# Retention: the first head's query handled inside the norm, values ahead of context keys, weight splits behind the rows that wait

## What is computed

```
hn, gn = pre_norm(h), pre_norm(g)              # latent, context
q = rotary(hn @ Wq);  k = rotary(hn @ Wk) / 16;  v = hn @ Wv;  gate = hn @ Wg
k_c = gn @ Wk / 16;   v_c = gn @ Wv
per head (4 heads, key width 256, value width 512):
    s_fwd, s_bwd = decayed sums of k_c x v_c   # state from the context
    o = scan(q, k, v, decay 0, s_fwd) + flipped scan(q, k, v, decay 1, s_bwd, strict)
    y = groupnorm(o) * gain * silu(gate);  h += mod * (y @ Wo)
```

## Time and profile before

| | us |
|---|---|
| median of 3 timed runs | 3056.75 (3056.71 to 3057.57) |
| the profiled execution | 3057.61 |
| its span | 3055.9 |

### The profile page before, as it was taken

How to read it: one execution, slowest core, us unless ns; L and a number is a source line. 1 busy time by engine, 2 the same in 40 slices (tenths; PEclk the granted TensorE clock), 3 DMA queues, 4 the chain that set the end, 5 groups by cost and what they waited for, 6 DMA issues and landing times.

```text
span 3055.9 us, 42286 instructions
## 1 busy us (share of the span) xinstructions
PE 2994.7 (98%) x17472; PEld 2608.9 (85%) x17472; DVE 1806.0 (59%) x2615; ACT 859.9 (28%) x1150; POOL 37.3 (1%) x74
## 2 busy tenths in 40 slices
PE   7999999999999999999999999999899999999999
PEld 5888888888898888888888888888788888888887
DVE  5765555766667775555673565658464646464454
ACT  5111121354445411121241121213332322332221
POOL 0000000000000000000000000000000000000000
PEclk9999999999999999999999999999999999999999
DMA  6332332111110333232311232321121212112222
GB/s 266 140 131 100 110 110 96 55 53 56 56 53 31 148 126 112 110 106 100 110 70 56 96 110 96 110 96 68 42 83 42 74 49 83 55 70 96 96 96 83
DMA packets 41064, 278.08 MB, mean 91 GB/s; under 512 B 4368, under 2 KB 5648, under 8 KB 8080
## 3 DMA queue, kind: packets, MB, share of 16 engines
q1 hardware_dynamic: 31024, 205.85, 18.6%
q0 software_dynamic: 9952, 70.98, 6.5%
HBM read 274.72 MB, written 2.10 MB: 91 GB/s over the span
## 4 chain that ended last, share of the span: by engine, by line
PE 90%; DVE 6%; ACT 2%; issue 1%; DMA 1%; SPq 0%; POOL 0%; DVEq 0%; ACTq 0%; POOLq 0%
PE ps L330 29%; PE ps L332 28%; PE ps L331 28%; PE ps L652 1%; PE ps L356 1%; DVE wl L1372 1%; DVE act_buf L1456 1%; DVE xnl L1460 1%; ACT wh L965 1%; DMA ada_w<-ada 1%; PE ps L344 1%; PE ps L638 0%; DMA adaw<-ada 0%; PE ps L639 0%; ACT xnh L996 0%
## 5 line engine op out<-in xcount | busy, mean ns | idle before, releaser
L330 PE MATMUL ps<-xnh,wl 128*128 128x512 f32 (+1 forms) x3040 | 1058.2, 348 | 12.3 <-DVE wl L1372 5.5
L331 PE MATMUL ps<-xnl,wh 128*128 128x512 f32 (+1 forms) x3040 | 1048.4, 345 | 0.0
L332 PE MATMUL ps<-xnh,wh 128*128 128x512 f32 (+1 forms) x3040 | 1047.5, 345 | 0.0
L330 PEld LDWEIGHTS ps<-xnh,wl 128*128 128x128 f32 x3040 | 577.2, 190 | 95.0 <-issue 10.7
L332 PEld LDWEIGHTS ps<-xnh,wh 128*128 128x128 f32 x3040 | 577.0, 190 | 70.1
L331 PEld LDWEIGHTS ps<-xnl,wh 128*128 128x128 f32 x3040 | 577.4, 190 | 67.7 <-issue 1.0
L965 ACT ACTIVATE wh<-raw 128x2048 fp32r<-128x2048 f32 (+2 forms) x176 | 322.7, 1834 | 560.8 <-PE ps L332 560.8
L1372 DVE TENSOR_TENSOR wl<-raw,wh 128x2048 fp32r<-128x2048 f32 (+1 forms) x178 | 393.6, 2211 | 139.8 <-ACT wh L965 139.6
L1529 DVE SCALAR_TENSOR_TENSOR h<-ps,coef,h 128x512 f32<-128x512 f32 x624 | 371.3, 641 | 106.1 <-PE ps L332 104.7
L330 PE MATMUL ps<-hidh,wl 128*128 128x512 f32 (+1 forms) x1232 | 422.4, 343 | 3.5 <-DVE h L1471 3.3
L332 PE MATMUL ps<-hidh,wh 128*128 128x512 f32 (+1 forms) x1232 | 423.2, 344 | 0.0
(11 more groups left out here) (255 smaller groups left out, 2973.4 us busy)
## 6 DMA issues: line engine op xcount, KB each, us to landing
raw<-weights SPq DMA_DIRECT2D x183, 1024.0 KB, 4.8
adaw<-ada POOLq DMA_DIRECT2D x64, 1024.0 KB, 5.0
ada_w<-ada SPq DMA_DIRECT2D x8, 1024.0 KB, 19.2
h<-x_in SPq DMA_DIRECT2D x1, 2048.0 KB, 8.7
c_act<-c_rows POOLq DMA_DIRECT2D x2, 1024.0 KB, 5.8
out<-h SPq DMA_DIRECT2D x8, 256.0 KB, 2.0
h<-x_in SPq DMA_DIRECT2D x1, 1024.0 KB, 28.9
cs<-rope_mla POOLq DMA_DIRECT2D x1, 512.0 KB, 3.7
```

The source lines that it names most:

```text
L330: mm(dst, lhs[1][rows], rhs[0][rows], start=first, stop=False)
L331: mm(dst, lhs[0][rows], rhs[1][rows], start=False, stop=False)
L332: return mm(dst, lhs[0][rows], rhs[0][rows], start=False, stop=last)
```

## The change

The first head's query is split, rotated and split again **between the two parts of the norm** instead of behind both: `last_y` gets a function `between`, which ScalarE calls ahead of `norm_hi` of part 1 and VectorE ahead of `normed` of part 1. In the first head TensorE multiplies **two value sets ahead of the context keys**, the second of them into bank 0, since bank 7 still holds the norm's spread; a wait for the query (`qk_ready`) stands in front of it. VectorE and ScalarE take the latent keys and the first value ahead of the decays, and the second value and the context keys behind them. Latent and context keys signal `qk_full` apart. In **all heads** ScalarE makes the context keys' high halves ahead of the split of the second value weights, VectorE makes the first value's low half ahead of that split and the decays' add, and the split of the gate weights stands behind the scores on both engines. The buffers `rk`, `st`, `rv`, `rq` change places, so that `rq` no longer lies over the norm's `act_buf`.

The diff; `rotate` is moved out of `head` unchanged and left out, as are the functions that hand `between` on and the loops' counts:

```diff
         mla_mem.close()
         ret_mem = ExitStack()
+        rk = sb("rk", [P, 2, 2, T], F32R, ret_mem)
+        st = sb("st", [P, 2, 6, S], F32R, ret_mem)
+        rv = sb("rv", [P, 2, 6, 256], F32R, ret_mem)
         rq = sb("rq", [P, 2, 2, S], F32R, ret_mem)
-        rk = sb("rk", [P, 2, 2, T], F32R, ret_mem)
-        rv = sb("rv", [P, 2, 6, 256], F32R, ret_mem)
-        st = sb("st", [P, 2, 6, S], F32R, ret_mem)
...
-                for i, (t0, n) in enumerate(STREAMS):
+                def keys(part):
+
+                    t0, n = STREAMS[part]
                     for j in range(2):
                         for k in range(KD):
-                            if first and not i and j and k == 4:
+                            if first and not part and j and k == 4:
                                 norm_spread(1)
-                            if first and i and j == 0:
+                            if first and part and j == 0:
                                 pe.wait_ge(xn_ready, c.next(xn_ready))
-                            ins = three(ps[:, 2 + 2 * i + j, 0:n], w(s1, k * 256 + j * P), xn(k, t0, n), k == 0, k == KD - 1)
-                        if first and i == 0 and j == 0:
+                            ins = three(ps[:, 2 + 2 * part + j, 0:n], w(s1, k * 256 + j * P), xn(k, t0, n), k == 0, k == KD - 1)
+                        if first and not part and j == 0:
                             norm_sums(1)
-                ins.then_inc(qk_full, 1)
+                    ins.then_inc(qk_full, 1)
+                keys(0)
+                if not first:
+                    keys(1)
                 pe.wait_ge(w_ready[s0], c.next(w_ready[s0]))
                 values(s0, 6, 0)
-                values(s0, 7, 1)
+                if first:
+                    pe.wait_ge(qk_ready, c.next(qk_ready))
+                    values(s0, 0, 1)
+                    keys(1)
+                else:
+                    values(s0, 7, 1)
                 pe.wait_ge(v_ready, c.next(v_ready))
                 values(s0, 6, 2)
-                pe.wait_ge(qk_ready, c.next(qk_ready, 2))
+                pe.wait_ge(qk_ready, c.next(qk_ready, 2 if first else 3))
+                if first:
+                    pe.wait_ge(v_ready, c.next(v_ready))
                 for jc in range(6):
                     if jc >= 4:
...
-                pe.wait_ge(v_ready, c.next(v_ready, 2))
+                pe.wait_ge(v_ready, c.next(v_ready, 1 if first else 2))
...
                 norm_root(1, parts)
+                if between is not None:
+                    between()
                 for m in range(KD):
...
-            slot = ffn(2, slot, (1, 1))
-
-
-            s0, s1 = slot, 1 - slot
...
+            def first_query():
+                act.wait_ge(qk_full, c.next(qk_full))
+                split_hi(1 - slot)
+                for j in range(2):
+                    part(qk_val, qk_hi, rq[:, 0, j, :], rt[:, j, :])
+            slot = ffn(2, slot, (1, 1), between=first_query)
+
+
+            s0, s1 = slot, 1 - slot
...
-                act.wait_ge(qk_full, c.next(qk_full))
-                split_hi(s0)
-                for j in range(2):
-                    part(qk_val, qk_hi, rq[:, 0, j, :], rt[:, j, :])
+                def ctx_keys():
+                    act.wait_ge(qk_full, c.next(qk_full))
+                    fn(rk[:, 0, 0, S:T], ps[:, 4, 0:L], ACT.Copy)
+                    fn(rk[:, 0, 1, S:T], ps[:, 5, 0:L], ACT.Copy).then_inc(qk_hi, 1)
+
+                def rows(kind):
+                    for j in range(2):
+                        part(qk_val, qk_hi, kind(j), rt[:, j, :])
+
+                def value(t):
+                    bank = 0 if first and t == 1 else 6 + t % 2
+                    part(v_full, v_hi, rv[:, 0, 2 * t:2 * t + 2, :], two_tiles(bank))
+                first = isinstance(i, int) and i == 0
+                if first:
+                    act.wait_ge(qk_full, c.next(qk_full))
+                    rows(lambda j: rk[:, 0, j, 0:S])
+                    value(0)
+                else:
+                    act.wait_ge(qk_full, c.next(qk_full))
+                    split_hi(s0)
+                    rows(lambda j: rq[:, 0, j, :])
                 act.wait_ge(dec_done, c.next(dec_done))
                 fn(dec_lat, dec_lat, ACT.Exp)
                 fn(dec_ctx, dist[:, L:DIST_W], ACT.Exp, bias=lg[:, 5, at(i)], scale=lgf)
                 fn(far[:], dist[:, L:DIST_W], ACT.Exp, bias=lg[:, 6, at(i + RET_HEADS)], scale=nlgb).then_inc(dec_exp, 1)
-                act.wait_ge(qk_full, c.next(qk_full))
-                split_hi(s1)
-                fn(rk[:, 0, 0, S:T], ps[:, 4, 0:L], ACT.Copy)
-                fn(rk[:, 0, 1, S:T], ps[:, 5, 0:L], ACT.Copy).then_inc(qk_hi, 1)
-                for j in range(2):
-                    part(qk_val, qk_hi, rk[:, 0, j, 0:S], rt[:, j, :])
-                for t in range(3):
-                    part(v_full, v_hi, rv[:, 0, 2 * t:2 * t + 2, :], two_tiles(6 + t % 2))
-                split_hi(s0)
+                if first:
+                    value(1)
+                    ctx_keys()
+                    split_hi(s1)
+                else:
+                    act.wait_ge(qk_full, c.next(qk_full))
+                    ctx_keys()
+                    split_hi(s1)
+                    rows(lambda j: rk[:, 0, j, 0:S])
+                    value(0)
+                    value(1)
+                value(2)
                 for jc in range(6):
                     part(sc_val, sc_hi, st[:, 0, jc, :], rt[:, jc % 2, :])
+                split_hi(s0)
                 act.wait_ge(o_full, c.next(o_full, 2))
                 for t in range(3):
                     part(v_full, v_hi, rv[:, 0, 2 * t:2 * t + 2, :], two_tiles(2 + t % 2))
...
@@ -1518,6 +1559,8 @@
                 inverse_rms(1, parts)
                 if early is None:
                     gate_coefs(layer, k)
+                if between is not None:
+                    between()
                 normed(1, layer, k, parts)
 
...
+            def query(s):
                 dve.wait_ge(qk_full, c.next(qk_full))
-                split_lo(s0)
+                split_lo(s)
                 rotate(0)
                 for j in range(2):
                     dve.wait_ge(qk_hi, c.next(qk_hi))
                     ins = tt(rq[:, 1, j, :], rt[:, j, :], rq[:, 0, j, :].bitcast(F32), ALU.subtract)
                 ins.then_inc(qk_ready, 1)
...
+            def first_query():
+                dve.wait_ge(tab_full, 48)
+                query(1 - slot)
+            slot = ffn(2, slot, (1, 1), ADA_2, between=first_query)
...
+                def ctx_keys():
+                    dve.wait_ge(qk_full, c.next(qk_full))
                     dve.wait_ge(qk_hi, c.next(qk_hi))
-                    ins = tt(rk[:, 1, j, 0:S], rt[:, j, :], rk[:, 0, j, 0:S].bitcast(F32), ALU.subtract)
-                ins.then_inc(qk_ready, 1)
-                split_lo(s1)
-                dve.wait_ge(dec_exp, c.next(dec_exp))
-                step(tt(dec_ctx, dec_ctx, far[:], ALU.add))
+                    for j in range(2):
+                        ins = tt(rk[:, 1, j, S:T], ps[:, 4 + j, 0:L], rk[:, 0, j, S:T].bitcast(F32), ALU.subtract)
+                    ins.then_inc(qk_ready, 1)
+
+                def other_keys():
+                    dve.wait_ge(qk_full, c.next(qk_full))
+                    dve.wait_ge(qk_ready, c.next(qk_ready, 1 if first else 2))
+                    rotate(2)
+                    for j in range(2):
+                        dve.wait_ge(qk_hi, c.next(qk_hi))
+                        ins = tt(rk[:, 1, j, 0:S], rt[:, j, :], rk[:, 0, j, 0:S].bitcast(F32), ALU.subtract)
+                    ins.then_inc(qk_ready, 1)
...
-                for t in range(3):
-                    value(t, 6 + t % 2)
-                split_lo(s0)
-                dve.wait_ge(qk_ready, c.next(qk_ready))
+                first = isinstance(i, int) and i == 0
+                if not first:
+                    query(s0)
+                else:
+                    other_keys()
+                    value(0, 6)
+                step(ts(dec_lat, dist[:], nlgb, None, ALU.mult))
+                stt(out=dec_lat, in0=dist[:], scalar=lgf, in1=dec_lat, op0=ALU.mult, op1=ALU.min).then_inc(dec_done, 1)
+                if first:
+                    value(1, 0)
+                    ctx_keys()
+                else:
+                    ctx_keys()
+                    other_keys()
+                    value(0, 6)
+                split_lo(s1)
+                dve.wait_ge(dec_exp, c.next(dec_exp))
+                step(tt(dec_ctx, dec_ctx, far[:], ALU.add))
+                if not first:
+                    value(1, 7)
+                value(2, 6)
+                dve.wait_ge(qk_ready, c.next(qk_ready, 2 if first else 1))
...
@@ -1912,6 +1978,7 @@
                         dve.wait_ge(sc_hi, c.next(sc_hi))
                         tt(st[:, 1, jc - 1, :], rt[:, (jc - 1) % 2, :], st[:, 0, jc - 1, :].bitcast(F32),
```

(50 more changed lines are left out.)

14 lines of the change are left out of this document (2 added, 12 removed).

## The result

| | before | after |
|---|---|---|
| median us (4 runs each) | 3056.73 (3055.35 to 3057.57) | 3028.98 (3028.00 to 3030.22) |
| ratio | | 0.9913, 95% interval 0.9902 to 0.9925 |
| the profiled execution, us | 3057.61 | 3029.51 |
| its span | 3055.9 | 3027.9 |

Faster by 27.7 us.

A forecast was written before the change was run, and what follows sets the result against it. TensorE, busy 98% of the span, was taken as the bound, so only its gaps could be won. First head 15.3 plus other heads 7.7 made 23.0 us, giving 3034 us; range 3032 to 3041.5.

The forecast's parts named there:

- The first head: Term for the first head: moving the query and reordering TensorE brings its fifth score block 15.3 us earlier.
- The wait for the first value: First head, TensorE waiting for the low half of `rv`: 10.2 us, forecast to shrink to about 0.1.
- the chain of ten pieces: First head, VectorE and ScalarE durations added in program order: scores at 2161.3, with a new 0.5 us wait before them.
- the pause of 1.3 us: First head, TensorE's pause before the fifth score block: 1.3 us by the trace, forecast to stay.
- The low clock: First head, third value set slowed at 1.2 GHz after the pause: 2.3 us lost, forecast to be recovered.
- The other heads: Heads two to four: waits for the first value and before the fifth score block go, 2.6 us each, 7.7 in all.
- the extra signal: Separate signal for the keys, forecast to cost nothing that a row could show.
- from the sum to the time: Last step: 23.0 us off the profiled 3057.61, then 0.86 off for the median: 3033.8, say 3034.
- (a): Rival, chance 0.10: only the first head gains, another wait takes over in the steady heads; 3041.4 us.
- (b): Rival, chance 0.07: the first head's chain is longer than added up; 6 us longer, with low clock, gives 3042 us.
- (c): Rival, chance 0.03: the value wait just becomes the same wait for context keys; 3056.75 us or a little less.
- (d): Rival, chance 0.04: slower, the first head's delayed second norm part becomes the bound; about 3063 us.

The follow-up runs named there:

- e6: Changed kernel, but in the first head TensorE takes the context keys ahead of the two value sets again; median 3039.23 us, ratio 0.9951.
- e3: Kernel before the change, with 42 never-read products filling TensorE's 10.2 us pause in the first head; median 3051.84 us, ratio 0.9992.
- e1: Changed kernel with only the first head's edits, heads two to four in the order of before; median 3041.3 us, ratio 0.9952.
- e5: Changed kernel keeping only the gate-weight split behind the scores in heads two to four, all else in the old order; median 3049.51 us, ratio 0.9986.
- e10: The changed kernel run a third time, nothing altered; median 3030.45 us, ratio 0.9919.
- e2: Changed kernel with the first head back in the order of before, heads two to four as changed; median 3046.84 us, ratio 0.9972.
- e7: Changed kernel, but the first head's query is handled behind both parts of the norm; TensorE's new order stays; median 3039.61 us, ratio 0.9951.

## Why the prediction was right or wrong

**The first head: right.** The query block took 2131.12 to 2138.70, 7.6 us (7.65 forecast), and nothing on its way was slower than in its old place. The norm's second part was put off by 5.9 us against the latent keys (6.1), with no wait on TensorE; e6 shows what the cover is worth, 7.7 us. The wait for the first value is gone. The term is 0.45 us too small, nearly all of it ahead of the scores. They start 35.98 us behind the first key product, and 2161.3 - 2124.93 = 36.4 had been forecast: the chain of ten pieces came out 0.3 shorter, so the new wait is 0.2 us instead of 0.5, and TensorE was ready a little earlier too. From there to the fifth block it is 6.72 us. The forecast had 2168.1 - 2161.3 = 6.8, which is less than the 6.97 of the earlier trace rows already, so its words that the pause of 1.3 us stays didn't fit its own sum; it fell to 0.9.

**The low clock: right.** The 2.3 us went with the pause (2.2 in e3); the granted clock was 1.00 throughout the stretch.

**The other heads: mechanism right, size 0.9 us short.** 1.7 and 1.2 us per head instead of 1.48 and 1.1. The waits themselves were right: from the scores to the fifth block it is 5.49 us instead of 6.97, the 1.48 exactly. What the term left out is the restart behind each wait. The last two score blocks take 2.72 us instead of 2.91, and the third value set 5.76 instead of 5.86; the prediction names that 0.1 itself and doesn't count it in. Three times 0.3 is the 0.9. The first value was ready 3.7 us ahead of TensorE (4), and the later split of the gate weights met nobody. My "costs nothing" for the extra signal was right for this kernel only: e1 and e5 show 0.2 us per head where the slack is missing.

**The step that failed is the last one, from the sum to the time.** "It lay 0.86 above the median of the timed runs, so the median should be 3033.8": this takes the median of three runs for the kernel's own level and gives the work outside the heads no spread. Three medians of 15 to 20 runs each put before at 3054.2 to 3055.0. The profiled execution that I worked from held one stretch at low clock at 20 to 30 us and two behind the heads, which come and go from execution to execution in either kernel; 3.7 us of the 28.1 lie outside the heads. From 3054.9 the true 24.4 give 3030.5, which is the median of e10. The sum of 23.0 was 1.35 short, the base 1.9 us high, and the four runs of the result lay 1.5 below 3030.5: with the rounding of 0.25 these are the 5.0 us of the miss. Why the base was 1.9 high stays open, as said above; the 1.5 are within the spread of the changed kernel, whose ten later runs lie between 3028.5 and 3033.7. The low end of the range, 3032, was built from the waits alone and so had no room for this.

**The rivals.** (a) fell: no other wait came up in heads two to four (e2, e5). (b) fell: the chain was shorter, not longer. (c) fell: the wait for context keys that took the place of the old one is 0.2 us. (d) didn't come up, as the norm's second part ended 0.4 us ahead of the context keys; in e6, where the keys come first, its mechanism costs 7.7 us.

## What to carry to other kernels

When TensorE meets a chain of converting engines, add up each engine's program in its order with the durations of the old place: this gave 15.3 for 15.75 us over ten pieces. A block moved ahead puts off what it passes. Here the query's place alone and the new order alone each brought about half (e6, e7), and each left the wait that the other removes. Before the sum becomes a time, look whether the profiled execution is a typical one: compare stretches that the change doesn't touch in more than one execution, and give the range their spread.

## What was not expected of the hardware

The granted clock at one place of one kernel is not the same in each execution. Over the five profiles of the two kernels it was 0.77 in three and 0.89 in two between 995 and 1010 us, and 0.83 in two and 1.00 in three between 20 and 30 us, with the same program. TensorE has waits in or ahead of these places: 15.4 to 15.7 us at the start, 3.0 us between 980 and 1015, and 2.8 and 2.0 us behind the heads. They are the same in all five profiles, so they alone don't decide whether the lower level follows. A pause of 4.9 us on TensorE (e6) was followed by the lower level, as were those of 8.7 (e7) and 10.2; behind the waits of 0.8, 0.2 and 0.9 us in the changed kernel's first head it stayed at the upper one. And 42 products whose result nobody reads (e3) kept it at the upper one.
